# One layer's mLSTM recurrence run a step ahead, its elementwise work divided anew over VectorE and ScalarE

## The reference

```
qa, ka, va, qm, km, vm, om, gates = jnp.split(h @ w_in, AB_SPLITS, axis=-1)
a_out = na_latent(...)                      # 8 attention heads
m_out = mlstm_mixer(...)                    # 4 mLSTM heads, both directions
out = jnp.concatenate([a_out, m_out], axis=-1) @ w_out
```

```
w_inter = jnp.exp(a - m_t)
Wd = jnp.exp(Dm - m_t[..., None])
s = jnp.einsum('bhtd,bhsd->bhts', qb, kb) * Wd
num = w_inter[..., None] * jnp.einsum('bhtd,bhde->bhte', qb, C) + jnp.einsum('bhts,bhse->bhte', s, vb)
den = w_inter * jnp.einsum('bhtd,bhd->bht', qb, n) + jnp.sum(s, axis=-1)
h = num / jnp.maximum(jnp.abs(den), jnp.exp(-m_t))[..., None]
C_new = wi_last[..., None, None] * C + jnp.einsum('bhs,bhsd,bhse->bhde', w_last, kb, vb)
```

## Time and profile before

| | us |
|---|---|
| median of 3 runs (2679.70 to 2679.85) | 2679.81 |
| the profiled execution, its own time | 2681.27 |
| its span | 2679.4 |
| PE busy in the span | 2585.8 (97%) |
| DVE, ACT, POOL busy | 1482.0, 670.0, 160.3 |
| mean granted clock of PE | 0.981 |

### The profile page before, as it was taken

The page is one execution under the profiler, slowest core; times in us unless marked ns, Lnnn a source line. Parts: engine busy times, 40 slices in busy tenths (PEclk is TensorE's granted clock), DMA queues, the critical chain, the costliest instruction groups (busy, mean ns, idle before and its releaser), DMA issues. The chain is left out here.

```text
span 2679.4 us, 40845 instructions
## 1 busy us (share of the span) xinstructions
PE 2585.8 (97%) x15572; PEld 2386.1 (89%) x15572; DVE 1482.0 (55%) x2599; ACT 670.0 (25%) x1170; POOL 160.3 (6%) x263
## 2 busy tenths in 40 slices
PE   7999999999999699999999999999999999999998
PEld 3998999799998579988997998899899979989997
DVE  3787588634444658864885887233454453332333
ACT  3121111443333143111113321121331142211122
POOL 1000000201111220000001000000110020000001
PEclk8999999999998799999999999999999999999999
DMA  6454445223210033533453353223312222222232
GB/s 216 134 153 126 131 148 173 88 73 81 57 47 13 11 112 118 157 110 116 144 168 107 103 149 125 79 71 94 95 49 78 93 72 65 77 71 79 72 105 82
DMA packets 381554, 270.56 MB, mean 101 GB/s; under 512 B 38892, under 2 KB 349420, under 8 KB 381452
## 3 DMA queue, kind: packets, MB, share of 16 engines
q1 hardware_dynamic: 381454, 269.21, 33.3%
HBM read 264.80 MB, written 4.30 MB: 100 GB/s over the span
## 5 line engine op out<-in xcount | busy, mean ns | idle before, releaser
L1479 DVE TENSOR_TENSOR w_lo<-w_raw,w_hi 128x1024 fp32r<-128x1024 f32 (+1 forms) x401 | 397.0, 994 | 638.5 <-ACT w_hi L1077 635.0
L752 PE MATMUL psum<-hT_hi,w_hi 128*128 128x320 f32 x3040 | 694.1, 310 | 2.1 <-DVE w_lo L1479 1.3
L752 PE MATMUL psum<-hT_lo,w_hi 128*128 128x320 f32 x3040 | 693.7, 309 | 0.0
L752 PE MATMUL psum<-hT_hi,w_lo 128*128 128x320 f32 x3040 | 693.5, 309 | 0.0
L1077 ACT ACTIVATE w_hi<-w_raw 128x1024 fp32r<-128x1024 f32 (+1 forms) x401 | 349.5, 873 | 1019.2 <-PE psum L752 536.7
L752 PEld LDWEIGHTS psum<-hT_hi,w_hi 128*128 128x128 f32 x3040 | 508.2, 188 | 3.6 <-issue 1.5
L752 PEld LDWEIGHTS psum<-hT_hi,w_lo 128*128 128x128 f32 x3040 | 508.5, 188 | 0.0
L752 PEld LDWEIGHTS psum<-hT_lo,w_hi 128*128 128x128 f32 x3040 | 508.4, 188 | 0.0
L1452 DVE SCALAR_TENSOR_TENSOR mod_acc<-ada_raw,cond_silu,mod_acc 128x256 f32<-128x256 f32 x896 | 365.5, 480 | 0.0
L690 PE MATMUL psum<-w_hi,act_hi 128*128 128x512 f32 x800 | 318.1, 398 | 10.5 <-DVE w_lo L1479 10.5
L692 PE MATMUL psum<-w_hi,act_lo 128*128 128x512 f32 x800 | 316.6, 396 | 0.0
(11 more groups left out here) (199 smaller groups left out, 2515.3 us busy)
## 6 DMA issues: line engine op xcount, KB each, us to landing
w_raw<-in_ffn_w_dram SPq DMA_DIRECT2D x176, 512.0 KB, 4.0
ada_raw<-in_ada_w_dram SPq DMA_DIRECT2D x128, 512.0 KB, 3.6
w_raw<-in_ffn_w_dram SPq DMA_DIRECT2D x148, 256.0 KB, 2.7
w_raw<-in_ab_w_in_dram SPq DMA_DIRECT2D x28, 512.0 KB, 4.1
w_raw<-in_sc_w_in_dram SPq DMA_DIRECT2D x24, 512.0 KB, 4.0
ada_first<-in_ada_w_dram SPq DMA_DIRECT2D x8, 1024.0 KB, 12.6
held_raw<-in_ffn_w_dram SPq DMA_DIRECT2D x28, 256.0 KB, 3.8
gate<-modulation SPq DMA_DIRECT2D x6, 1024.0 KB, 6.1
```

The lines of the kernel that those rows point to most:

```text
L752: last = mm(IN[p][0:width, h, 0:HT], a, b[:, k, h * HT:(h + 1) * HT], start=(k == 0 and a is hi and b is hT_hi), stop=(k == KD - 1 and a i ...
L1479: V.tensor_tensor(d_, a, b.bitcast(F32), ALU.subtract).then_inc(w_lo_ok, 1)
```

## The change

- PE runs `front(q + 2)` ahead of `back(q)`; DVE runs `decay(q + 2)`, then the scores of q + 1 (`score`), then `finish(q)`, then the weighted queries of q + 1 (`scale_q`).
- The weighted queries go from POOL to DVE (one instruction of 128x512), the weighted values from POOL to ACT (four of 128x129), the squares of the heads from DVE to ACT (four of 128x128 with an accumulator). `decay` and the sum into `h_sum` become four instructions of 128x128 each in place of two of 128x512.
- Output weights 1 to 5 are loaded and split during and just after the recurrence (`AB_SPLIT`), weights 6 to 11 behind the gate as before. The mixer's held weights get a place of their own, `held_ab`, and no longer wait for the activations. It overlaps `ada_raw`, so SP waits for the end of the sublayer before (`out_last`) ahead of the first `ada_raw` load of a first FFN half.
- The output projection starts on the attention channels; the heads are turned inside it, at channels 3, 4 and 5 (`turn_heads`), and `act_ready` is given head by head.
- In both sublayers with eight units the gate product moves from unit 4 to 6 and the held splits from units 5 to 8 to units 6 to 9.

```diff
+        held_of = lambda ph, i: held_ab[i] if ph.get("ab") else (held_hi[i], held_lo[i], held_raw[i])
+        SPLIT_HELD = {HF: (5, 8, 11, 11, 12, 12, 13), KD: (6, 7, 8, 9)}
+        AB_SPLIT = 6
...
                 if jobs:
                     load_bias(ph)
+                    need(sp, out_last, 0 if ph["half"] else ph["sub"])
                     load_job(ph, 0)
                     body(2)
...
                             dma(Cs[:, dr, :, MLD:MLD + 1], state_n[0, 0, dr].rearrange("h (p a) -> p h a", a=1), **slow).then_inc(st_loaded, 16)
+                        load_out(s, ab_w_out[0], 0, ph, 1, AB_SPLIT)
...
-                        load_out(s, ab_w_out[0], 0, ph, 1)
+                        load_out(s, ab_w_out[0], 0, ph, AB_SPLIT)
...
+                        if ph.get("ab"):
+                            if t == NT - 1:
+                                pe.wait_ge(ml_x, len(ML_STEPS) - 1)
+                                pe.wait_ge(ml_wi, len(ML_STEPS) - 1)
+                            elif t < 2:
+                                pe.wait_ge(ml_h, len(ML_STEPS))
+                            else:
+                                pe.wait_ge(ml_cs, len(NEEDS_STATE))
...
-                    for t in range(NT):
+                    if turns is not None and d == 0 and k in (3, 4, 5):
+                        turns({3: (0, 1), 4: (2,), 5: (3,)}[k])
+                    for t in ((NT - 1, 0, 1, 2, 3) if ph.get("ab") and k == 0 else range(NT)):
...
-                for q in range(len(ML_STEPS) + 1):
-                    if q < len(ML_STEPS):
-                        front(q)
-                    if q:
-                        back(q - 1)
-
-                pe.wait_ge(h_n_ok, NT)
-                for h in range(MLH):
+                front(0)
+                front(1)
+                for q in range(len(ML_STEPS)):
+                    if q + 2 < len(ML_STEPS):
+                        front(q + 2)
+                    back(q)
+
+            def turn_heads(heads):
+                if heads[0] == 0:
+                    pe.wait_ge(h_n_ok, NT)
...
+                for h in heads:
                     if h >= 2:
                         pe.wait_ge(hT2_evac, h - 1)
...
@@ ScalarE @@
                 for q, (dr, cc) in enumerate(ML_STEPS):
                     act.wait_ge(ml_x, q + 1)
+                    A(Wx[:, q % 2], Wx[:, q % 2], ACT.Exp, scale=-1.0).then_inc(ml_w, 1)
...
-                        act.wait_ge(ml_h, q - 1)
                         act.wait_ge(ml_qs, min(q - 1, 8))
-                        act.wait_ge(ml_vw, sum(1 for z in NEEDS_STATE if z < q - 1))
                         act.wait_ge(ml_cs, sum(1 for z in NEEDS_STATE if z < q - 1))
...
-                    A(Wx[:, q % 2], Wx[:, q % 2], ACT.Exp, scale=-1.0).then_inc(ml_w, 1)
+                    if q in NEEDS_STATE:
...
+                        for h in range(MLH):
+                            last = A(vw[:, j % 2, h, :], vmt[:, cc, h, :], ACT.Copy, scale=Wx[:, q % 2, h, edge:edge + 1])
+                        last.then_inc(ml_vw, 1)
+                    if q - 2 in whole_at:
+                        head_squares(whole_at.index(q - 2))
+                    if q in (1, 3, 5):
+                        split(ph["nout"] + (q + 1) // 2, shape="out", u=(q + 1) // 2)
+                head_squares(NT - 1)
+                for u in range(4, AB_SPLIT):
+                    split(ph["nout"] + u, shape="out", u=u)
...
@@ VectorE @@
-                    own.link(V.tensor_tensor(Wx[:, q % 2], rm, e, ALU.subtract))
-                    V.tensor_tensor(Wx[:, q % 2], Wx[:, q % 2], mlmask[:, dr, None, :].to_broadcast([P, MLH, P]), ALU.add).then_inc(ml_x, 1)
+                    for h in range(MLH):
+                        last = V.scalar_tensor_tensor(Wx[:, q % 2, h, :], rm[:, h, :], ecol[:, 0, dr, cc, h:h + 1], mlmask[:, dr, :], ALU.subtract, ALU.add)
+                    last.then_inc(ml_x, 1)
...
+                        V.tensor_tensor(qs[:, q % 2], FT[:, 8:12, cc * P:(cc + 1) * P], wi[:, q % 2], ALU.mult).then_inc(ml_qs, 1)
+
                 decay(0)
-                done = 0
+                decay(1)
+                score(0)
+                scale_q(0)
                 for q in range(len(ML_STEPS)):
+                    if q + 2 < len(ML_STEPS):
+                        decay(q + 2)
                     if q + 1 < len(ML_STEPS):
-                        decay(q + 1)
+                        score(q + 1)
                     finish(q)
...
+                    if q + 1 < len(ML_STEPS):
+                        scale_q(q + 1)
+                    if q - 2 in whole_at:
+                        head_scale(whole_at.index(q - 2))
+                    if q in (1, 3, 5):
+                        split(ph["nout"] + (q + 1) // 2, shape="out", u=(q + 1) // 2)
+                head_scale(NT - 1)
+                for u in range(4, AB_SPLIT):
+                    split(ph["nout"] + u, shape="out", u=u)
```

More of the change, by code:

```diff
@@ L235, in build @@
             held_raw.append(at(f"held_raw{3 + i}", [P, KD, TOK], where[name])[:, 4:8, tok])
+        held_ab = []
+        for i in range(HELD[KD]):
+            z = arena + 20 * TOK * 4 + i * 4096
+            held_ab.append((at(f"held_ab_hi{i}", [P, 4, P], z, F32R)[:], at(f"held_ab_lo{i}", [P, 4, P], z + 2048, F32R)[:],
+                            at(f"held_ab_raw{i}", [P, 4, P], z + 2048)[:]))
+        held_of = lambda ph, i: held_ab[i] if ph.get("ab") else (held_hi[i], held_lo[i], held_raw[i])
         FT = at("featT", [P, 20, TOK], arena)
@@ L357, in build @@
                     iv = ev.phase(b, FFN_IN)
-                    ph.append(dict(nin=b, iv=iv, iv_end=list(ev.n), nout=b + FFN_IN, oe=oe, ar=ar, k=HF, half=h, held=HELD[HF] * h,
+                    ph.append(dict(sub=s, nin=b, iv=iv, iv_end=list(ev.n), nout=b + FFN_IN, oe=oe, ar=ar, k=HF, half=h, held=HELD[HF] * h,
                                    jobs=JOBS[s][2][h] if s in JOBS else 0, late=JOBS[s][3][h] if s in JOBS else 0, jb=jb,
@@ L369, in build @@
                 iv = ev.phase(b, AB_UNITS + 1)
-                ph = [dict(nin=b, iv=iv, iv_end=list(ev.n), nout=b + AB_UNITS + 1, oe=oe, ar=ar, k=KD, held=HELD[KD])]
+                ph = [dict(nin=b, iv=iv, iv_end=list(ev.n), nout=b + AB_UNITS + 1, oe=oe, ar=ar, k=KD, held=HELD[KD], ab=True)]
                 oe += 2 * NT
@@ L1162, in out_splits @@
                 K, units = ph["k"], out_units(ph)
-                for u in range(1, len(units)):
+                for u in range(AB_SPLIT if ph.get("ab") else 1, len(units)):
                     split(ph["nout"] + u, shape="out", u=u)
-                    for i in (i for i in range(ph["held"]) if min(LOAD_HELD[K][i] + 2, len(units) - 1) == u):
-                        split_held(s, i)
+                    for i in range(ph["held"]):
+                        if SPLIT_HELD[K][i] == u:
+                            split_held(s, ph, i)
                 if final:
@@ L1307, in mixing, with head_squares @@
                 A(FT[:, 16:20, :], FT[:, 16:20, :], ACT.Sigmoid).then_inc(om_ok, 1)
+                whole = [z[1] for q, z in enumerate(ML_STEPS) if z[1] in [y[1] for y in ML_STEPS[:q]]]
+                whole_at = [q for q, z in enumerate(ML_STEPS) if z[1] in [y[1] for y in ML_STEPS[:q]]]
+                def head_squares(n):
+                    act.wait_ge(ml_h, whole_at[n] + 1)
+                    if n:
+                        act.wait_ge(h_ssq_ok, n)
+                    c4 = whole[n] * MLH
+                    for h in range(MLH):
+                        last = A(htmp[:, h, :], hsum[:, whole[n], h, :], ACT.Square, accum_out=hssq[:, c4 + h:c4 + h + 1])
+                    last.then_inc(h_ssq_ok, 1)
                 for q, (dr, cc) in enumerate(ML_STEPS):
                     act.wait_ge(ml_x, q + 1)
+                    A(Wx[:, q % 2], Wx[:, q % 2], ACT.Exp, scale=-1.0).then_inc(ml_w, 1)
                     if q == 0:
@@ L1603, in out_phase @@
                 final = ph is plan[s][-1]
-                for u in range(1, len(units)):
+                for u in range(AB_SPLIT if ph.get("ab") else 1, len(units)):
                     split(ph["nout"] + u, shape="out", u=u)
-                    if final and u == 4:
+                    if final and u == (4 if K == HF else AB_SPLIT):
                         gate_tile(s)
-                    for i in (i for i in range(ph["held"]) if min(LOAD_HELD[K][i] + 2, len(units) - 1) == u):
-                        split_held(s, i)
+                    for i in range(ph["held"]):
+                        if SPLIT_HELD[K][i] == u:
+                            split_held(s, ph, i)
                     z, r = divmod(u - 1, 3)
@@ L1868, in finish @@
                     own.link(V.reciprocal(dn, dn))
-                    r_ = den[:, q % 2, :, None].to_broadcast([P, MLH, MLD])
                     if cc in seen:
-                        own.link(V.tensor_tensor(htmp[:], num[:, :, 0:MLD], r_, ALU.mult))
```

(13 more changed lines are left out.)

89 lines of the change are left out of this document (45 added, 44 removed).

## The result

| | before | after |
|---|---|---|
| median, us | 2679.83 (2679.70 to 2684.33, 4 runs) | 2642.83 (2640.52 to 2644.58, 4 runs) |
| profiled execution: own time; span | 2681.27; 2679.4 | 2644.58; 2642.5 |
| mean granted clock | 0.981 | 0.989 |

The ratio of the times is 0.9857, 95% interval 0.984 to 0.9874: 37 us less. The forecast was 2646 in a range of 2640 to 2660.

A forecast was written before the change was run, and what follows sets the result against it. The recurrence's chain over PE and DVE, then a 15.2 us tail, bound the kernel. Terms -24.2 (recurrence), -15.2 (tail), +2.8 (turning), +2.6 (split 11) sum to -34.0: 2646 us from the median, range 2640 to 2660.

The forecast's parts named there:

- What bounds: Recurrence, 839.6 to 925.2 us: each step a chain over PE and DVE, 6.4 us at full clock; POOL not binding.
- The opening: Start of the recurrence: `front(2)` ahead of `back(0)` costs 4.0 us at half the clock; first divisor at 854.0.
- The steps: Ten recurrence steps, divisor to divisor: 5.15 us for a plain one, more with splits or whole chunks; sum 44.5 us.
- the two are matched: Recurrence step: PE's list ends at 5.1 us and DVE's queries at 5.0, giving a step of 5.15 us.
- The allowance of 2.5 us: Added for the clock to the end of the recurrence's last sum: 901 in place of 898.5 us.
- The rival of half the clock: Recurrence steps with PE held at half its clock, 9 us for 5.15: 2661 or 2671 us; chance 0.15.
- Tail and projection: Behind the last sum PE passes straight into the projection: 15.2 us saved, 2.8 for turning and 2.6 for split 11 lost.
- The ring of weights: Projection weights 8 to 11, each loaded two splits behind: split 11 ends 36 us after the last sum, when PE wants it.
- The end is set by the chain behind the split of 11: End of the projection: that chain, not PE, sets the end; split at 938 us, gain 34 us.
- ScalarE last: Recurrence steps: ScalarE becomes the last if its small instructions cost a third more, 2651 to 2661 us; chance 0.08.
- Weights 6 to 11 late: Projection: DVE splits them behind head 3, SP loads them behind the stores; up to 7 us, 2653 us; chance 0.05.
- Slower: Recurrence loop closes over everything, 12.2 us a step at half the clock, 2695 us; chance 0.02.

The follow-up runs named there:

- e2: Changed kernel with only the recurrence's order undone (`front`, decay, scores and queries one step ahead as before): 2667.23 us, ratio 0.9949.
- e1: Changed kernel with both multiplications, weighted queries and weighted values, back on POOL, the new order kept: 2639.15 us, ratio 0.9842.
- e7: Changed kernel with only the weighted queries back on POOL, the values staying on ACT: 2639.10 us, ratio 0.9838.
- e5: Changed kernel with DVE's split of output weight 6 ahead of head 3 and the gate product behind unit 9: 2641.28 us, ratio 0.9851.
- e6: Changed kernel with weight 6 split ahead of head 3, gate product behind unit 9, and first-half copy ahead of split 11: 2636.23 us, ratio 0.9835.
- a0: The changed kernel run again without any edit: 2641.03 us, ratio 0.9846.
- e10: Changed kernel with ScalarE's weighted values computed a second time into a tile nobody reads: 2641.48 us, ratio 0.9856.

## Why the prediction was right, step by step

**What bounds.** Right: the step was a chain over both engines because decay and scores stood behind `finish` (e2). That POOL did not bind is shown for the new order (e1, e7); in the old one its products and the larger instructions together cost at most some 4 of 84 us (e2).

**The opening.** Forecast 14.4 us from `front(0)` to the first divisor, measured 13.16 (855.92 - 842.76). `front(2)` cost its 4.0 us at half the clock (3.9 measured), but the first row of stabilisers ran at the full clock (1.12 us for 2.04 before), and PE no longer waited 0.44 for the scores.

**The steps.** Forecast 5.15, 5.3, 5.15, 5.3, 5.65, 5.8, 4.8, 3.0, 2.6, 1.7; measured 5.09, 5.10, 5.09, 5.09, 5.53, 5.53, 4.49, 3.05, 2.61, 1.74. Sum 43.3 for 44.5. The loop that closes is the one named, numerator, divisor, `h_sum`, state, queries. A split on DVE costs nothing in steps 1 and 3, because it stands in the time in which DVE would wait for the numerator; I had charged 0.15 each. But "the two are matched" was half right: PE's list alone is 4.85, and the move of the queries to DVE is why it is not reached. That the move of the queries, a part of what the change is named after, is a loss in this order, I did not see.

**The clock.** The allowance of 2.5 us was not needed: 1.00 from 855.3 on. The rival of half the clock fell with it; e2 shows that it was real for another order. The rival's first sentence read the rows wrongly: the clock did not fall whenever PE had idled. In the kernel before, PE waited 1.0 to 1.3 us ahead of four numerators in steps 1 to 4, which then took 2.09 us three times and 3.70 once; only in steps 5 to 7, behind waits of 3.3 to 3.7 us, did all three take 3.49 us or more.

**Tail and projection.** With T for the end of the last sum, 899.24: the first product starts at 898.11, the heads are done at T + 21.8 (forecast 23.2), weight 6 is issued at T + 13.9 and rounded at T + 18.2 (13 and 18), the split of 11 is done at T + 34.2 (36 and 1 of allowance). The ring of weights, not PE, sets that split; e5 shows 2.35 us in it. The prediction's sum had PE and ring end together and held this cost only as a rival.

**From there on.** "The end is set by the chain behind the split of 11": right, 15.2 to 15.4 us in all kernels but e6. Missed: PE's list now ends 6.0 us ahead of the turned tile, not 3.2, its clock falls to half, and the way from the tile to the third split is 40.8 us for 39.4: 1.4 given back.

**The rest.** The new wait costs nothing: the `ada_raw` load goes out at 968.01 and is used at 986.01 without a wait. The gate product one unit later costs nothing against before, but is in the ring (e5).

**The sum.** From `front(0)` to the copy the change gave 41.7 us (132.32 to 90.61), where the prediction had 34.0. Of the 7.7 us between them 1.2 are the opening, 1.2 the steps, 2.5 the clock, 2.8 the projection. Given back are 1.4 us in the boundary to the next FFN and 3.2 ahead of `front(0)`. The 3.2 are chance: a0, the same kernel, has its `front(0)` at 839.28, and the kernel before at 839.59. 41.7 - 1.4 - 3.2 = 37.1; the spans differ by 36.9. So 2646 was 3 us from the median with a recurrence and projection that were 7.7 us too long, and more than half of that was offset by a loss that the prediction did not have and by chance. The mechanism was right and the sizes a little pessimistic; that the number came so near is in part luck.

**The rivals.** Half clock in the steps: no. ScalarE last: no, and not even with 1.2 us more in each step (e10). Weights 6 to 11 late: yes in part, 2.35 us by e5, hidden in the sum by the allowance. Slower: no.

## What to carry to other kernels

When two engines wait for each other in turn, the first thing to change is the order. Undoing it alone took 25 of the 37 us back: the waits themselves were the larger part, and 9 to 12 us were clock that the waits had cost. Moving work to a faster engine pays only if the slow engine is on the chain. In the new order a product of 1.29 us on POOL was free and one of 0.68 on DVE cost 0.24 a step; in the old order the same move, with smaller instructions, had still gained, by up to 4 us. After each gain look for the next gap: two changes to DVE's list in the projection were worth another 3.4 us, and then five products on POOL held the chain. To see differences of that size, read each trace from a landmark just ahead of the change.

## What the runs showed of the hardware

- The clock at the opening. PE idles 1.98 us before `front(0)`, then works without a gap from 842.76 on. The row of stabilisers takes 1.12 us for eight, from 844.90 on 2.05, and the clock is at 0.50 until about 855: ten us of half clock with PE busy in all of it. Windows of the changed kernel:

```profile
843.00:845.00 2.00, 2.00 (x17) 1.76 (x16) 1.08 (x4) 2.00 (x1) 0.00 (x0) 0.99 0.92 192
845.00:847.00 2.00, 2.00 (x9) 1.77 (x9) 0.06 (x2) 1.97 (x3) 0.00 (x0) 0.50 0.60 222
...
853.00:855.00 2.00, 2.00 (x11) 2.00 (x11) 0.00 (x0) 0.10 (x1) 0.00 (x0) 0.50 0.00 0
855.00:857.00 2.00, 2.00 (x17) 1.88 (x17) 0.97 (x4) 0.00 (x0) 0.00 (x0) 0.95 0.00 0
```

  The Trainium skill ("TensorE: Matmul & The Clock Gate", what is actually happening) says that activity releases the throttle. Here the throttle stayed on through ten us of work without a gap; why was not tried.
- Two executions of the same kernel differ by the number of times that the clock falls to 0.50. The same wait of 2.4 us was followed by a fall in one and by none in the other, and a fall in otherwise full work cost 1.54 us; two of them made 3.08 of the 3.48 us between the two at `front(0)`. Why it falls in one execution and not in the other stays open.
- Where a product of two SBUF tiles on DVE and one on POOL, both 128x512, overlapped, one of them was longer: POOL's 1.84 us for 1.29 (e6), or DVE's 1.51 for 0.69 (the changed kernel). Why was not tried.
- Four ScalarE copies of 128x129 with a scale from a column take 1.28 us, four exponentials of 128x128 out of PSUM 1.14. The same product of 128x516 is one instruction on POOL, listed with 1.05 us.
